# A decoder layer on one core: the samples' softmax and value products moved into the attention loop

## The chip, the cores and the metric

One core of a Trainium2 chip runs the whole kernel. The metric is the device time of one execution in microseconds (us), as the median of several; lower is better. All data are 32-bit floats. The engines are TensorE (PE), VectorE (DVE), ScalarE (ACT), GpSimd (POOL), and SyncE (SP), which only issues transfers here. Each runs its own instructions in the order written and waits on semaphores for the others.

## What is computed

One transformer layer for a prompt of 512 tokens and for 8 samples, each with one new token and a paged cache of 2048 past positions (16 pages of 128). Cut to what the change touches:

```python
proj = rmsnorm(x) @ w_in            # gates, u, v, q, k, v_c, forget
y_a = short_conv_mixer(...)         # z = c * h, three taps, gate
y_b = chunk_gmlp_mixer(...)         # layernorm(v), w_s, gate u
y_c = fox_prompt(q, k, v, logf)     # causal attention of the prompt, 8 heads, head size 64
# the samples instead attend to the cache:
s_past = einsum('nqhd,nkhd->nhqk', q, k_past) * scale + decay
s_new = einsum('nqhd,nkhd->nhqk', q, k) * scale + ...
p = softmax(concatenate([s_past, s_new]))
o = einsum(p_past, v_past) + einsum(p_new, v)
x = x + concatenate([rmsnorm(y_a), rmsnorm(y_b), rmsnorm(y_c)]) @ w_o
x = x + hier_moe(rmsnorm(x))        # 32 experts, 6 MB of weights each, top 2
x = x + (p_i @ w_ple) * sigmoid(rmsnorm(x) @ w_ple_gate)
```

## The kernel before

The program is one hand-ordered instruction list per engine. Its stages, in order:

1. **Projections and keys.** The input is normalised and transposed, and `project` (L1229, matmuls at L1237) forms half of the projections. Beside it the samples' keys are read from the cache in 32 chunks of 1 MB (128 pages, 4 key positions of 512 numbers) by indirect DMAs on GpSimd (`load_chunk`, L656, issue at L659) into a ring of six slots. Of the first `SHARED` = 24 chunks GpSimd multiplies the even ones by the query (`products`, L689) and VectorE the odd ones (`key_pair`, L1796); VectorE sums all (`reduce_keys`, L1786, instruction at L1791). Behind pairs 9 and 10 VectorE also copies the prompt's values out of PSUM (`copy_values`, L1838).
2. **Attention of the prompt.** A loop of 17 steps (`STEPS` = 16), step s working on heads 2c, 2c+1 and query block t, with c, t = s // 4, s % 4. TensorE runs `query_keys(s)` (L1318), the rest of the projections in pieces (`rest_step`, L1301, matmuls at L1313), `transpose_p(s-1)` (L1328), spreads a head's decay row over the partitions into PSUM bank 7 (`spread_ck`, L1288) or puts the values of the gating there (`spread_gv`, L1292), and at every fourth step runs `weigh_values` (L1340, matmuls at L1352) into bank 6. `CK_STEP` and `GV_STEP` say at which steps bank 7 is so used. VectorE masks and takes maxima (`negate_scores`, L1899), inverts the sums (`invert_sums`), reads bank 7 (`diagonal`, `layer_stats`, and once `layer_norms`, L1877), and sums the last eight key chunks at the steps in `REDUCE_AT`. ScalarE takes the exponentials and copies. Value chunks 0 to 3 of the cache are loaded as the four slots of the ring come free; GpSimd then builds constants and waits.
3. **Norms.** VectorE forms the convolution (`z` at L1947, taps L1954 to L1964) and the gates (L1977, L1980), TensorE the sums of squares (L1403) and the spread roots (L1413), VectorE the normalised rows (L1988). SP loads `w_o` (4 MB, L544) when the last query-key product is out and the prompt's x again (2 MB, L548) behind the last `weigh_values`.
4. **Output product, samples and routing.** `mix_out(t)` (L1450, matmuls at L1462) forms the output product of token tile t in four quarters of 4 matmuls; a matmul of 32-bit floats shows as two rows of the trace, so a quarter is 8 rows. VectorE takes the samples' softmax (L2012 to L2033) behind the norms; `values_step(i)` (L1388) forms four chunks of the samples' value product each, 8 matmuls (16 rows, L1383) into bank 7 per chunk, one accumulation over all 32 chunks. VectorE writes each chunk's probabilities, spread over the samples, into one of four buffers (`spread_p`, L2034). The load of chunk n waits for the product of chunk n - 4. `add_out` adds x, `second_norm` (L2062) takes the root on VectorE in ten instructions (`root`, L1733) and normalises, and `route(t)` (L1467) forms the routing logits. Then follow the samples' output (`oN`, L1523), the remaining tiles, the embedding product (L1567) and the lists of rows per expert.
5. **Experts.** 32 experts in a loop; SP streams each one's 6 MB into one of two buffers (L554, L555, L558). Expert 0's first 4 MB wait for the last value product, expert 1's for the last `mix_out`, the later ones for the expert before (matmuls at L1611 and L1626).
6. **Gate, last norm, stores** (matmuls at L1719).

The fills of banks 4 and 5 alternate in the order of the list `FILLS` (L86): a fill waits until the one before it in its bank is read. Bank 7 holds the decay rows in the attention and, when all are read, the sum of the value products.

## Time and profile before

| what | value |
|---|---|
| median of 3 runs | 1093.56 us (1087.73 to 1096.13) |
| profiled execution, its own time | 1092.19 us |
| its span in the trace | 1090.4 us |
| granted clock over the span | 0.896 |
| PE busy | 886.6 us (81%) |
| DVE, ACT, POOL busy | 334.0, 193.2, 264.0 us |
| HBM traffic | 297 GB/s over the span |

The span runs from the first to the last recorded instruction; 1.8 us of the execution lie around it. Times of rows count from the span's start. A PE row's clock is the share of 2.4 GHz that was granted, so 1.00 is 2.4 GHz and 0.50 is 1.2 GHz.

### The profile page before, as it was taken

The page shows a single profiled execution, that of the slowest core. Times are in us where ns is not written, and L with a number is a line of the kernel's source. Part 1 is how long each engine was busy: PE and PEld are TensorE (multiplying, and loading weights), DVE is VectorE, ACT ScalarE, POOL GpSimd, SP SyncE. Part 2 cuts the span into 40 slices and gives each one's busy share as a digit, 9 for nine tenths or more (in the row PEclk, how much of TensorE's full clock was granted, in tenths as well). Part 3 has the DMA queues.
Part 4 walks back from the last instruction along what each step waited for, and adds up shares of the span by engine and source line. Part 5 has one row for each costly group of instructions (what it writes and reads, how often), then busy time and mean ns, then how long its engine had stood idle before and what let it go on. Part 6 is the DMA issues. An engine that isn't in the chain of part 4 may idle for free.

```text
span 1090.4 us, 11578 instructions
## 1 busy us (share of the span) xinstructions
PE 886.6 (81%) x4285; PEld 465.3 (43%) x4285; DVE 334.0 (31%) x672; ACT 193.2 (18%) x391; POOL 264.0 (24%) x333
## 2 busy tenths in 40 slices
PE   5999689998697779768997787787787887885895
PEld 3888456767543335333333233333333333331342
DVE  4897456464651222460000000000000000000652
ACT  3200234544100000211101101101101101110432
POOL 6889249400012220002111111101111111001110
PEclk9999879999598898888988888988988989998898
DMA  9899526316028986705999999999999999997300
GB/s 310 320 336 372 202 95 232 119 37 243 10 83 328 399 328 238 303 5 181 404 408 415 397 402 410 409 404 413 409 412 414 405 397 413 424 404 297 150 40 38
DMA packets 53799, 316.42 MB, mean 290 GB/s; under 512 B 11214, under 2 KB 24078, under 8 KB 33016
## 3 DMA queue, kind: packets, MB, share of 16 engines
q1 hardware_dynamic: 34704, 233.28, 53.7%
q0 software_dynamic: 14480, 76.17, 18.5%
q10 hardware_dynamic: 4576, 6.46, 1.7%
q8 instruction: 24, 0.39, 0.1%
q14 instruction: 15, 0.12, 0.0%
HBM read 309.31 MB, written 14.82 MB: 297 GB/s over the span
## 4 chain that ended last, share of the span: by engine, by line
PE 48%; DMA 36%; DVE 8%; POOL 2%; issue 2%; ACT 2%; SPq 1%; POOLq 0%; DVEq 0%; ACTq 0%
DMA arena<-in_w_up 29%; PE psum L1611 14%; PE psum L1237 6%; PE psum L1719 5%; PE psum L1313 5%; PE psum L1462 5%; DMA arena<-in_cache_v,indices 4%; PE psum L1383 2%; DMA arena<-in_w_in 1%; DMA arena<-in_w_down 1%; POOL arena L692 1%; DVE arena L1791 1%; PE psum L1567 1%; PE psum L1626 1%; PE psum L1325 1%
## 5 line engine op out<-in xcount | busy, mean ns | idle before, releaser
L1611 PE MATMUL psum<-arena 128*64 128x512 f32 x1024 | 269.6, 686 | 86.4 <-DMA arena<-in_w_up 86.4
L1611 PEld LDWEIGHTS psum<-arena 128*64 128x64 f32 x1024 | 92.2, 157 | 239.7 <-issue 237.6
L2238 DVE TENSOR_TENSOR arena<-arena,psum 64x512 f32<-64x512 f32 x32 | 22.1, 692 | 385.3 <-ACT arena L1095 385.3
L1626 PE MATMUL psum<-arena 128*64 128x512 f32 x512 | 116.0, 592 | 2.1 <-DMA arena<-in_w_down 2.1
L692 POOL TENSOR_TENSOR arena<-arena 128x2048 f32<-128x2048 f32 x20 | 90.6, 4534 | 1.8 <-ACT arena L854 1.4
L1237 PE MATMUL psum<-arena 128*128 128x260 f32 x384 | 85.1, 383 | 0.2 <-DMA arena<-in_w_in 0.2
L746 POOL COPY indices<-row_list 128x1 int32 (+1 forms) x26 | 4.6, 178 | 307.0 <-ACT arena L1101 307.0
L1095 ACT ACTIVATE arena<-psum 64x512 f32<-64x512 f32 x32 | 18.8, 588 | 336.4 <-PE psum L1611 336.4
L1313 PE MATMUL psum<-arena 128*128 128x260 f32 x320 | 78.1, 398 | 0.0
L1237 PEld LDWEIGHTS psum<-arena 128*128 128x128 f32 x384 | 72.6, 190 | 12.3 <-issue 1.3
L1791 DVE TENSOR_REDUCE arena<-arena 128x32 f32<-128x2048 f32 x32 | 72.0, 2281 | 5.8 <-POOL arena L692 5.3
L1626 PEld LDWEIGHTS psum<-arena 128*64 128x64 f32 x512 | 42.0, 137 | 69.6 <-issue 68.9
L659 POOL DMA_INDIRECT arena<-in_cache_v,indices x32 | 32.2, 1006 | 158.9 <-PE psum L1383 152.3
L1313 PEld LDWEIGHTS psum<-arena 128*128 128x128 f32 x320 | 60.7, 195 | 17.4 <-issue 6.0
L1462 PE MATMUL psum<-arena 128*128 128x512 f32 x128 | 65.0, 662 | 1.8 <-DVEq L1731 1.8
L1719 PE MATMUL psum<-arena 128*128 128x512 f32 x128 | 55.7, 593 | 0.0
L747 POOL DMA_INDIRECT moe_rows<-arena,indices x32 | 32.6, 1019 | 94.8 <-ACT arena L1101 67.7
L1383 PE MATMUL psum<-arena 128*32 128x256 f32 x512 | 37.9, 441 | 18.6 <-DMA arena<-in_cache_v,indices 15.5
L659 POOL DMA_INDIRECT arena<-in_cache_k,indices x32 | 30.9, 965 | 45.5 <-DVE arena L1791 38.8
L1462 PEld LDWEIGHTS psum<-arena 128*128 128x128 f32 x128 | 26.4, 214 | 36.3 <-issue 34.2
L2242 DVE COPY arena<-psum 128x256 f32<-128x256 f32 x32 | 13.6, 425 | 86.4 <-PE psum L1619 86.4
L740 POOL DMA_INDIRECT arena<-h_rows,indices x32 | 31.2, 975 | 26.6 <-POOL indices L739 25.9
(320 smaller groups left out, 872.3 us busy)
## 6 DMA issues: line engine op xcount, KB each, us to landing
arena<-in_w_down SPq DMA_DIRECT2D x32, 2048.0 KB, 25.6
arena<-in_w_gate SPq DMA_DIRECT2D x31, 2048.0 KB, 18.3
arena<-in_w_up SPq DMA_DIRECT2D x31, 2048.0 KB, 22.8
arena<-in_w_in SPq DMA_DIRECT2D x11, 1024.0 KB, 6.9
arena<-in_x_prompt SPq DMA_DIRECT2D x8, 512.0 KB, 5.9
arena<-in_w_o SPq DMA_DIRECT2D x1, 4096.0 KB, 14.0
arena<-in_w_ple_gate SPq DMA_DIRECT2D x1, 4096.0 KB, 24.5
arena<-moe_rows SPq DMA_DIRECT2D x4, 1024.0 KB, 7.9
```

Of the source, the lines that this page charges most:

```text
L659: pool.indirect_dma_start(ring[s], None, caches[cache], bass.IndirectOffsetOnAxis(ap=chunk_ids[:, n:n + 1], axis=0)).then_inc(kv_in[s], 16)
L692: pool.tensor_tensor(r, r, q_rep, ALU.mult).then_inc(kmul, 1)
L740: pool.indirect_dma_start(h_rows[s][0:SLOTS, :], None, h2_dram, bass.IndirectOffsetOnAxis(ap=tok_ix[s][0:SLOTS, 0:1], axis=0), bounds_chec ...
L747: return pool.indirect_dma_start(moe_dram, bass.IndirectOffsetOnAxis(ap=row_ix[s][:, 0:1], axis=0), y_rows[s], None, bounds_check=2 * PAIR ...
L1237: last = mm(psum[:, 2 * q + half, 0:HALF], w_ring[s][:, k, q * P:(q + 1) * P], hT[:, k, half * HALF:(half + 1) * HALF], start=(k == 0), st ...
L1313: last = mm(bank(4 + half)[:, 0:HALF], w_ring[g % 2][:, k, q * P:(q + 1) * P], hT[:, k, half * HALF:(half + 1) * HALF], start=(k == 0), st ...
L1383: ins = mm(bank(7)[32 * g:32 * (g + 1), 0:WA], p_exp[s][:, k * HC + 4 * half:k * HC + 4 * half + 4, :], ring[s][:, k * WC + half * WA:k * ...
L1462: last = mm(bank(2 * (t % 2) + n)[0:w, :], heads, w_out[:, k, n * BANK:(n + 1) * BANK], start=(k == 0), stop=(k == DC - 1))
L1611: last = mm(bank(s)[m * SLOTS:(m + 1) * SLOTS, :], hgT[s][:, k, :], w_gu[s][m][:, k, :], start=(k == 0), stop=(k == DC - 1))
L1626: last = mm(bank(6 + s)[n * SLOTS:(n + 1) * SLOTS, :], actT[s][:, k, :], w_dn[s][:, k, n * BANK:(n + 1) * BANK], start=(k == 0), stop=(k = ...
L1719: last = mm(bank(2 * (i % 2) + n), xT[i % 2][:, k, :], w_gate_ple[:, k, n * BANK:(n + 1) * BANK], start=(k == 0), stop=(k == DC - 1))
L1791: v.tensor_reduce(scores[:, n * KEYS * HC:(n + 1) * KEYS * HC], ring[SLOT[n]].rearrange("p (a d) -> p a d", d=HD), AX.X, ALU.add).then_inc ...
```

## The change

The samples' scores are taken to their maximum at attention step 3 (VectorE), the maxima are transposed and spread at steps 5 and 6 (TensorE in bank 6, VectorE), the exponentials are at step 6 (ScalarE), the sums at step 7. The value products of chunks 0 to 19 stand in steps 10 to 15; of the 12 left, 8 stand behind the loop, 2 behind the gates and 2 ahead of the spread of the norms. The decay rows and the gating's values are through bank 7 by step 9. The probabilities of a chunk are spread over the samples in one of eight buffers, which lie where the pages' forget logs and decays were. 28 instead of 24 key chunks are summed ahead of the attention, four in it. The copies of the prompt's values stand further back on VectorE, and the new token's score (three small VectorE instructions) stands ahead of the attention. The root of the second norm moves from VectorE to GpSimd (two instructions). Cut to its core:

```diff
-SHARED = 24
-V_AFTER = {9: (0, 1), 10: (2, 3)}
-REDUCE_AT = {24: (1, 0), 25: (1, 1), 26: (2, 1), 27: (3, 0), 28: (3, 1), 29: (4, 1), 30: (5, 1), 31: (6, 0)}
+SHARED = 28
+REDUCE_AT = {28: (1, 0), 29: (1, 1), 30: (2, 1), 31: (3, 0)}
+VALUES_AT = {10: (0, 1, 2, 3), 11: (4, 5, 6, 7), 12: (8, 9, 10), 13: (11, 12, 13), 14: (14, 15, 16), 15: (17, 18, 19)}
+SPREAD_AT = {7: (0, 1, 2, 3), 10: (4, 5, 6, 7), 11: (8, 9, 10), 12: (11, 12, 13), 13: (14, 15, 16), 14: (17, 18, 19),
+             15: (20, 21, 22)}
+EXPANDED = 8
-CK_STEP = {h: 4 * (h // 2 - 1) + 1 + h % 2 for h in range(2, HC)}
-GV_STEP = {3: 0, 4: 1, 7: 2, 8: 3, 11: 4}
+CK_STEP = {2: 0, 3: 1, 4: 4, 5: 5, 6: 8, 7: 9}
+GV_STEP = {3: 0, 4: 1, 6: 2, 7: 3, 8: 4}
...
-        p_exp = [at(b_tail + 4 * SEQ + s * KEYS * HC * NB, KEYS * HC, NB) for s in range(4)]
+        p_exp = [at(pages0 + s * KEYS * HC * NB, KEYS * HC, NB) for s in range(EXPANDED)]
```

GpSimd: key chunks and first value chunks:

```diff
             for n in range(0, SHARED, 2):
                 products(n)
-                if n:
+                if 0 < n < SHARED - 4:
                     pool.wait_ge(kred, n)
                     load_chunk(0, n + 4)
                     load_chunk(0, n + 5)
             for n in range(SHARED, CHUNKS):
+                pool.wait_ge(kred, n - 3)
+                load_chunk(0, n)
+            for n in range(SHARED, CHUNKS):
                 products(n)
-                if n > SHARED:
-                    pool.wait_ge(kred, n)
-                    load_chunk((n + 3) // CHUNKS, (n + 3) % CHUNKS)
-            pool.wait_ge(kred, CHUNKS)
-            load_chunk(1, 3)
+                if n >= SHARED + 2:
+                    pool.wait_ge(kred, n - 1)
+                    load_chunk(1, n - SHARED - 2)
+            for n in (2, 3):
+                pool.wait_ge(kred, SHARED + n + 1)
+                load_chunk(1, n)
```

GpSimd, after the last value chunk's load:

```diff
+            for t in sorted(TURN, key=TURN.get):
+                w = tile_width(t)
+                r = stats[0:w, 56 + t:57 + t]
+                pool.wait_ge(x1_ms, TURN[t] + 1)
+                step(pool.tensor_scalar(r, stats[0:w, 24 + t:25 + t], 1.0 / D, EPS, ALU.mult, ALU.add))
+                pool.tensor_tensor(r, r, minus_half[0:w, :], ALU.pow).then_inc(x1_root, 1)
```

ScalarE, attention loop:

```diff
+                if s == 6:
+                    act.wait_ge(smp_exp, 1)
+                    act.activation(scores, scores, ACT.Exp).then_inc(smp_p, 1)
+                    act.wait_ge(smp_exp, 2)
+                    act.activation(pnew[0:NB, :], new_s[0:NB, :], ACT.Exp).then_inc(smp_p, 1)
```

TensorE; weigh_values(c), c > 0, also waits smp_exp 2:

```diff
+            def values(n):
+                out = bank(7)
+                if n == 0:
+                    pe.wait_ge(gv_read, TILES)
+                    pe.wait_ge(ck_diag_ready, HC)
+                    pe.wait_ge(ck_ready, HC)
+                pe.wait_ge(kv_in[SLOT[CHUNKS + n]], arrived(CHUNKS + n))
+                pe.wait_ge(px_ready, n + 1)
+                p, v = p_exp[n % EXPANDED], ring[SLOT[CHUNKS + n]]
...
+            def sample_max(rows):
+                if rows:
+                    pe.wait_ge(a_of, 1)
+                    pe.wait_ge(smp_req, 1)
+                    tr(bank(6)[0:NB, P:P + HC], new_s[0:NB, :], ident[0:NB, 0:NB])
+                    tr(bank(6)[0:HC, 0:P], max_p, ident).then_inc(smp_full, 1)
+                else:
+                    pe.wait_ge(smp_req, 2)
...
             for s in range(STEPS + 1):
...
+                if s == 5:
+                    sample_max(True)
                 if s:
                     transpose_p(s - 1)
+                for n in VALUES_AT.get(s, ()):
+                    values(n)
...
+                if s == 5:
+                    sample_max(False)
                 if s and s % QT == 0:
                     weigh_values(s // QT - 1)
...
+            values_left(len(left) - 4)
+            wait_free(pe, "sum")
+            pe.wait_ge(smp_req, 3)
+            done(mm(fill("sum")[0:NB, 0:HC], col_sel, sum_p, start=True, stop=True), "sum")
             wait_free(pe, "state")
```

After the gates:

```diff
+            values_left(2)
```

After norm_sums("normB"):

```diff
+            values_left(len(left))
             spread_norm("normC")
...
-            mix_out(0, (0, 1, 2))
-            softmax_T("maxT", 1, slice(0, HC), max_p)
-            softmax_T("maxB", 2, slice(0, P), m_exp[0:HC, :])
-            softmax_T("maxN", 2, slice(0, NB), mT[0:HC, :])
-            mix_out(0, (3,))
-            mix_out(1, (0,))
...
-            values_step(0, first=True)
-            mix_out(1, (1,))
-            values_step(1)
-            mix_out(1, (2, 3))
-            values_step(2)
+            mix_out(0)
+            mix_out(1)
             route(0)
-            for m in range(4):
-                values_step(3 + m)
-                mix_out(2, (m,))
+            mix_out(2)
             route(1)
-            values_step(7, last_one=True)
```

VectorE, ahead of the attention:

```diff
-            for n in range(5, SHARED // 2):
+            for n in range(5, SHARED // 2 - 2):
                 key_pair(n)
-                for t in V_AFTER.get(n, ()):
-                    copy_values(t)
+            multiply_keys(SHARED - 3)
+            reduce_keys(SHARED - 4)
+            copy_values(0)
+            reduce_keys(SHARED - 3)
+            copy_values(1)
+            multiply_keys(SHARED - 1)
+            copy_values(2)
+            reduce_keys(SHARED - 2)
+            copy_values(3)
+            reduce_keys(SHARED - 1)
```

VectorE, attention loop, behind negate_scores(s):

```diff
+                if s == 5:
+                    sample_max_all()
+                if s == 6:
+                    sample_subtract()
+                if s == 7:
+                    sample_sums_p()
+                for n in SPREAD_AT.get(s, ()):
+                    spread_p(n)
```

Behind invert_sums(s):

```diff
+                if s == 3:
+                    sample_max()
```

VectorE, behind the attention:

```diff
+            for n in range(max(SPREAD_AT[max(SPREAD_AT)]) + 1, CHUNKS):
+                spread_p(n)
+            wait_full(dve, "sum")
+            dve.wait_ge(smp_p, 2)
+            step(v.tensor_tensor(sum_s[0:NB, :], fill("sum")[0:NB, 0:HC], pnew[0:NB, :], ALU.add))
+            dve.nop().then_inc(free_of("sum"), 1)
+            step(v.reciprocal(sum_s[0:NB, :], sum_s[0:NB, :]))
             dve.wait_ge(half_free, rest_halves - 4)
             z = projT[:, 2:4, :]
```

VectorE, second_norm(t):

```diff
-                dve.wait_ge(x1_ms, TURN[t] + 1)
-                root(stats[0:w, 56:57], stats[0:w, 24 + t:25 + t], 1.0 / D)
+                dve.wait_ge(x1_root, TURN[t] + 1)
```

## Rows read from the trace of the kernel before

**Rows 1.** Page, part 4: the chain that ended last, by line.

```profile
DMA arena<-in_w_up 29%; PE psum L1611 14%; PE psum L1237 6%; PE psum L1719 5%; PE psum L1313 5%; PE psum L1462 5%; DMA arena<-in_cache_v,indices 4%; PE psum L1383 2%; DMA arena<-in_w_in 1%; DMA arena<-in_w_down 1%; POOL arena L692 1%; DVE arena L1791 1%; PE psum L1567 1%; PE psum L1626 1%; PE psum L1325 1%
```

**Rows 2.** Busy time by stretch: the stretches are stages 2 to 5.

```profile
core 0: us, PE busy (x) PEld busy (x) DVE busy (x) ACT busy (x) POOL busy (x), PEclk, DMA share, GB/s
143.56:264.50 120.94, 115.78 (x551) 82.99 (x550) 61.39 (x203) 59.09 (x159) 46.42 (x75) 0.96 0.37 130
264.50:297.35 32.85, 21.34 (x134) 19.62 (x132) 21.95 (x58) 5.37 (x6) 0.00 (x0) 0.62 0.24 87
297.35:411.01 113.66, 91.14 (x662) 42.16 (x663) 35.72 (x85) 6.88 (x12) 28.33 (x28) 0.87 0.71 278
495.35:998.15 502.80, 412.16 (x1905) 164.50 (x1904) 35.73 (x64) 57.72 (x96) 69.65 (x118) 0.91 0.99 399
```

**Rows 3.** Groups by line, TensorE, 297 to 411 us.

```profile
L1383 PE MATMUL psum<-arena 128*32 128x256 f32 x512 | 37.9, 441 | 18.6 <-DMA arena<-in_cache_v,indices 15.5 <-DVE arena L2038 3.1
```

**Rows 4.** Timeline, TensorE: start, duration, line, shape, count, [idle before and releaser].

```profile
297.35 13.31 PE L1462 MATMUL psum<-arena 128*128 128x512 f32 x24 [1.78 <-DVEq L1731]
...
322.73 3.70 PE L1462 MATMUL psum<-arena 128*128 128x512 f32 x8
326.42 1.07 PE L1383 MATMUL psum<-arena 128*32 128x256 f32 x16
...
333.83 1.93 PE L1383 MATMUL psum<-arena 128*32 128x256 f32 x16 [2.63 <-DMA arena<-in_cache_v,indices]
...
403.13 1.95 PE L1482 MATMUL psum<-arena 128*128 128x36 f32 x16 [0.90 <-ACTq L1036]
```

**Rows 5.** Timeline, VectorE, ahead of the attention.

```profile
98.57 4.48 DVE L1791 TENSOR_REDUCE arena<-arena 128x32 f32<-128x2048 f32 x2
121.57 0.69 DVE L1840 COPY arena<-psum 128x512 f32<-128x512 f32 x1 [18.52 <-PE psum L1245]
...
124.01 2.29 DVE L1800 TENSOR_TENSOR arena<-arena,psum 128x2048 f32<-128x2048 f32 x1 [0.24 <-DVE arena L1840]
...
140.76 0.69 DVE L1894 SCALAR_TENSOR_TENSOR arena<-psum,arena 128x512 f32<-128x512 f32 x1
```

**Rows 6.** Timeline, TensorE, attention step 4.

```profile
179.41 3.98 PE L1352 MATMUL psum<-arena 128*64 128x512 f32 x16 [1.92 <-ACT arena L952]
```

**Rows 7.** Busy time by stretch: attention steps 10 and 16.

```profile
217.47:223.50 6.03, 6.03 (x27) 4.05 (x26) 2.52 (x11) 3.52 (x11) 0.00 (x0) 1.00 0.55 172
256.91:264.50 7.59, 6.85 (x42) 4.86 (x40) 0.00 (x0) 3.44 (x7) 0.00 (x0) 1.00 1.02 414
```

**Rows 8.** Timeline, SyncE's transfers: issue time, time in issue, line.

```profile
252.78 0.37 SPq L544 DMA_DIRECT2D arena<-in_w_o  x1
```

**Rows 9.** Timeline, VectorE, the norms.

```profile
255.54 1.22 DVE L1947 TENSOR_TENSOR arena<-arena 128x1040 f32<-128x1040 f32 x1
264.95 0.49 DVE L1956 TENSOR_SCALAR arena<-arena 128x520 f32<-128x520 f32 x1 [8.19 <-PE psum L1419]
...
275.71 0.69 DVE L1977 TENSOR_TENSOR arena<-psum,arena 128x512 f32<-128x512 f32 x1 [3.08 <-PE psum L1440]
...
278.95 0.68 DVE L1992 TENSOR_TENSOR arena<-arena 8x512 f32<-8x512 f32 x1
```

**Rows 10.** Timeline, TensorE, the norms.

```profile
267.21 5.60 PE L1403 MATMUL psum<-arena 128*128 128x1 f32 x32 [2.17 <-ACT arena L983]
...
280.01 3.57 PE L1403 MATMUL psum<-arena 128*128 128x1 f32 x16 [1.02 <-ACT arena L1001]
...
283.80 3.78 PE L1413 MATMUL psum<-arena 128*128 128x128 f32 x16
```

**Rows 11.** Timeline, VectorE, root and second norm of the samples' tile.

```profile
443.74 0.14 DVE L1738 TENSOR_SCALAR arena<-arena 8x1 f32<-8x1 f32 x1 [1.21 <-ACT arena L1019]
...
445.88 1.27 DVE L2068 SCALAR_TENSOR_TENSOR arena<-arena 8x1024 f32<-8x1024 f32 x1
```

**Rows 12.** One line's instructions: GpSimd's power at L641, min/median/max ns.

```profile
L641 POOL TENSOR_TENSOR arena<-arena x5: 553/556/857, 7.1 to 15.4; 128x1 f32<-128x1 f32 x4, 8x1 f32<-8x1 f32 x1
```

More of the change, by code:

```diff
@@ L88 @@
          + ["suffix"]
-         + ["state", "vnT", "z", "gate0", "gate1"]
-         + ["newT", "normC", "normA", "normB", "maxT", "maxB", "maxN"]
-         + ["sum"] + [f"h{t}{s}" for t in (0, 1) for s in "abr"] + ["oN", "oT"] + [f"h2{s}" for s in "abr"] + ["normS"]
+         + ["sum", "state", "vnT", "z", "gate0", "gate1", "normC", "normA", "normB"]
+         + [f"h{t}{s}" for t in (0, 1) for s in "abr"] + ["oN", "oT"] + [f"h2{s}" for s in "abr"] + ["normS"]
          + ["p01", "p23", "p4"] + [f"h{t}{s}" for t in (4, 3) for s in "abr"]
@@ L232, in build @@
         params_nat = small(P)
+        pages0 = small_top[0]
         logf_pages = small(PAGE, HC)
@@ L1354, in weigh_values @@
                 last.then_inc(a_o, 1)
+            def values(n):
[7 more added lines that the diff above has]
+                p, v = p_exp[n % EXPANDED], ring[SLOT[CHUNKS + n]]
+                for k in range(KEYS):
+                    for half in range(2):
+                        g = 2 * (k % 2) + half
+                        ins = mm(out[32 * g:32 * (g + 1), 0:WA], p[:, k * HC + 4 * half:k * HC + 4 * half + 4, :],
+                                 v[:, k * WC + half * WA:k * WC + (half + 1) * WA],
+                                 start=(n == 0 and k < 2), stop=(n == CHUNKS - 1 and k >= 2), skip_group_check=True)
+                ins.then_inc(pv_done, 1)
+            def sample_max(rows):
[6 more added lines that the diff above has]
+                    pe.wait_ge(smp_req, 2)
+                    tr(bank(6)[:, 0:HC], m_exp[0:HC, :], ident[0:HC, 0:HC])
+                    tr(bank(6)[0:NB, P:P + HC], mT[0:HC, :], ident[0:HC, 0:HC]).then_inc(smp_full, 1)
             spread_ck(0)
@@ L1371, in _ @@
                     spread_gv(GV_STEP[s])
+                if s == 5:
+                    sample_max(False)
                 if s and s % QT == 0:
                     weigh_values(s // QT - 1)
-            def values(s, loaded, spread, first=False, last_one=False):
-                pe.wait_ge(kv_in[s], loaded)
-                pe.wait_ge(px_ready, spread)
-                for k in range(KEYS):
-                    for half in range(2):
-                        g = 2 * (k % 2) + half
-                        ins = mm(bank(7)[32 * g:32 * (g + 1), 0:WA], p_exp[s][:, k * HC + 4 * half:k * HC + 4 * half + 4, :],
-                                 ring[s][:, k * WC + half * WA:k * WC + (half + 1) * WA],
-                                 start=(first and k < 2), stop=(last_one and k >= 2), skip_group_check=True)
-                ins.then_inc(pv_done, 1)
-            def values_step(i, **flags):
-                for s in range(4):
-                    values(s, arrived(CHUNKS + 4 * i + s), 4 * i + s + 1, flags.get("first", False) and s == 0,
-                           flags.get("last_one", False) and s == 3)
             pe.wait_ge(a_pt, 2 * STEPS)
@@ L1415, in spread_norm, with values_left @@
                 done(last, name)
+            left = list(range(max(VALUES_AT[max(VALUES_AT)]) + 1, CHUNKS))
+            def values_left(n):
+                for _ in range(n):
+                    values(left.pop(0))
+            values_left(len(left) - 4)
+            wait_free(pe, "sum")
+            pe.wait_ge(smp_req, 3)
+            done(mm(fill("sum")[0:NB, 0:HC], col_sel, sum_p, start=True, stop=True), "sum")
             wait_free(pe, "state")
@@ L1442, in _ @@
                 done(last, name)
-            def softmax_T(name, need, dst, src):
-                wait_free(pe, name)
-                pe.wait_ge(smp_req, need)
-                n = src.shape[0]
-                done(tr(fill(name)[dst, 0:n], src, ident[0:n, 0:n]), name)
+            values_left(2)
             def mix_out(t, quarters=(0, 1, 2, 3)):
@@ L1860, in _ @@
             dve.nop().then_inc(free_of("suffix"), 1)
+            for name in ("ks", "vs"):
+                dve.wait_ge(free_of(name), AT[name][1] + 1)
+            step(v.tensor_tensor(prod_s[0:NB, :], q_s[0:NB, :], k_s[0:NB, :], ALU.mult))
+            step(v.tensor_reduce(new_s[0:NB, :], prod_s[0:NB, :].rearrange("p (h d) -> p h d", h=HC), AX.X, ALU.add))
+            step(v.tensor_tensor(new_s[0:NB, :], new_s[0:NB, :], f_nat[0:NB, QT, :], ALU.subtract))
             step(v.memset(mv, 1.0))
```

116 lines of the change are left out of this document (43 added, 73 removed).

## The prediction

> **What bounds the kernel now.** I read the page's chain first. Its largest item is the transfer of the experts' weights, with the experts' matmuls behind it [rows 1]. The table of stretches says the same: over 502.8 us the DMA engines are busy 0.99 of the time at 399 GB/s, so the expert stage is a stream of 201 MB that nothing in this change touches [rows 2]. It starts when the routing lists are there, so a gain ahead of it moves the whole rest forward by its own size, and nothing else counts. Ahead of it the same table shows three stages of different kinds. In the attention TensorE is busy 115.8 of 120.9 us and DMA only 0.37. In the norms neither is full: 21.3 of 32.9 us and a granted clock of 0.62. In the output product, up to the samples' output, TensorE has 91.1 of 113.7 us at a DMA share of 0.71 [rows 2]. The groups by line say why: TensorE waited 15.5 us directly for value chunks and 3.1 us for VectorE ahead of the value products, and the chain gives these transfers 4% of the span, some 43 us [rows 1, 3]. So 32 chunks of 1 MB are loaded and used in a stage where they are the bound, while the DMA engines idle in the two stages before. The change moves them there. The question is how much TensorE and the transfers lose on the way.
>
> All sums are in the coordinates of the profiled execution (1092.19 us), which is 1.4 us under the median shown; I take the forecast made against it as the forecast of the median.
>
> **1. Ahead of the attention: -5.4 us.** VectorE ends key pair 9 at 103.05 us and then waits 18.5 us for the prompt's first transposed values; the first decay row is read at 140.76 [rows 5]. After the change two pairs' work stands in that gap. A pair is one product of 2.29 and a double sum of 4.48, 6.77 us [rows 5]. Pairs 10 and 11 end at 116.6, one product and one sum (2.24) at 121.1, just when the values come (121.57). Behind them come four copies of 0.69, three sums of 2.24 and one product, 11.8 us, to 133.4; page_suf 0.2; the new token's score, three instructions that took from 278.95 to 280.5 us, 1.55 [rows 9]; the memset 0.1. The decay row is read at 135.3 instead of 140.8. GpSimd's products are paced by the same pairs as now and hold nothing up; ScalarE's stores need the fourth copy, at 131 us, and are done by then.
>
> **2. Attention up to step 9: -1.5 us.** TensorE waits 1.92 us at step 4, behind VectorE, which waits for GpSimd's late key chunks [rows 6]. With four chunks left instead of eight, and GpSimd free of loads between their products, I let this and a smaller wait beside it go, -2.5. Four small transposes of the samples' maxima cost +1. The softmax adds to VectorE at step 3 about 4.5 us, at steps 5 to 7 some 5 us, and 32 spreads of 0.42 us; it loses four sums of 2.28. VectorE is busy 61.4 of 120.9 us [rows 2] and TensorE asks for each step's result a step later, so I take nothing; its other end is one late step, +3. The exponential on ScalarE (1 us, half idle there) is hidden too. GpSimd's building of constants stood in its long wait and moves ahead with the value loads, still ahead of step 10.
>
> **3. Steps 10 to 15: +21.4 us.** A chunk's product takes 1.07 us at the full clock [rows 4]; 20 of them are 21.4 us on an engine without gaps (step 10: 6.03 of 6.03 us, [rows 7]). Do the chunks arrive? Four lie ready. The DMA queue gave 414 GB/s when full [rows 7], so a chunk takes 2.53 us. Step 11 wants four chunks in some 11 us and the others three in 8 to 11 us, 7.6 us of transfer: they do. The ends are 0 and +6, a wait of 1 to 2 us in some steps for the first chunk of a refill. I take 0. So the last weigh_values ends at 264.6 - 5.4 - 1.5 + 21.4 = 279, I say 280.
>
> **4. The eight chunks behind the loop: done at 298.** This is where I expect the transfers to become late. w_o now goes out at 252.8 [rows 8], then at 252.8 - 6.9 + 17 x 1.07 = 264. The load of chunk n waits for product n - 4, so chunks 21 to 23 go out from 270 on. From 270 to the landing of chunk 27 the queue has to move the rest of w_o (4.2 MB less 5.5 us x 0.414 = 1.9 MB), chunks 21 to 27 (7.3 MB) and x (2.1 MB, out at 280): 11.3 MB, 27.4 us at 414 GB/s, so 297.4. TensorE alone would be through at 280 + 8 x 1.07 = 288.6. These are the ends if the value chunks went ahead of the others or came last. The profile shows the value loads only without such company. I take the late end, 298. The Trainium skill, "DMA: Bandwidth & Descriptors" (Queues, rings and completion order), says that each DMA engine serves its queues in turn, packet by packet; by that x and w_o land within the same stretch and the late end holds. The same page (Where 436 GB/s comes from) puts the HBM side at about 358 GB/s per core; the row with 414 disagrees, and by the page the time here would be 31.6 us, 4 us more.
>
> **5. From there to the output product: +38 us.** VectorE now gets to z only behind the sum of the exponentials, which TensorE forms behind chunk 27. So z, ready at 256.8 and hidden, moves onto the path: about 0.3 + 0.5 + 1.22 = 2 us [rows 9]. From the first tap (264.95) to mix_out (297.35) it is 32.4 us now [rows 4, 9]. Off go the new token's score, 1.55, and most of the 3.08 us that the gates waited for TensorE [rows 9], since its 5.60 us of sums [rows 10] now start before the taps. On come four chunks between the gates and the spread norms, on a TensorE that takes its sums of squares, 3.57 us, and the spread in turn [rows 10]: 4.3 us at the full clock, 7.7 at the half one, as the 1.93 us of a chunk behind a wait show [rows 4]; the stage runs at 0.62 [rows 2]. 2 + 32.4 - 1.5 - 2.9 + 4.3 = 34.3, or with the half clock for chunks and sums about 41; I take 38. The output product starts at 336 instead of 297.35: +38.7.
>
> **6. The output product: -57.2 us.** It is 113.66 us now [rows 2]. What stays: the first three quarters 13.31, nine quarters at 3.65 (a row shows 3.70) = 32.9, two routes of 4.0 (transposes 1.0, wait 0.90, product 1.95, [rows 4]). New is a wait ahead of the samples' output: VectorE reads bank 7 only behind add_out(2), the logits and the second norm, which the last four chunks covered; 1.28 + 0.42 and the hops, 2.3 us. Sum 56.5.
>
> **7. The root on GpSimd: -1.3 us.** The samples' tile waits on it ahead of its routing: VectorE takes 445.88 - 443.74 = 2.14 us [rows 11], GpSimd a power of 0.56 and a smaller instruction of 0.2 [rows 12]. The next tile's root lies behind the same path and gains no more. GpSimd waits for nothing else there.
>
> **The sum:** +38.7 - 57.2 - 1.3 = -19.8 us (points 1 to 4 are in the 336), 1092.2 - 19.8 = 1072.4. **1072 us**, its own range 1066 to 1080.
>
> **The rivals.** *The transfers are not late* (20%): chunks 21 to 27 get through ahead of w_o and x, TensorE ends chunk 27 at 289 and the norms take 34 to 36. 1072 less 9 to 13: 1061. For it: at step 10 DMA is at 0.55 [rows 7], over the whole attention at 0.37 [rows 2]. Against it: w_o and x must move in the same 30 us.
>
> *The value loads cost the attention too* (20%): four slots with a round trip through TensorE, GpSimd and the queue leave 1 to 2 us at each of steps 11 to 15, +6, and the norm stage runs at the half clock, +3, with 2 to 3 us of VectorE's softmax on the path. 1084. For it: chunk products waited 2.63 and more behind a refill in the old order [rows 4], on a full queue. A change that fails to do what it says would look so as well: products placed early that stand waiting.
>
> *Slower* (5%): the waits in steps 10 to 16 take TensorE to its half clock, and the projections and transposes there pay double. That stretch is 47 us with 44 of TensorE work, so at the half clock +44 us; the gain of 20 is gone when the clock is down in more than 45% of it, and for all of it the time is 1116. For it: the stages in which TensorE waits for others run at 0.62 and 0.87, the attention at 0.96 [rows 2]. Against it: the projections keep TensorE busy 4 us and more per step whatever the chunks do. The Trainium skill, "TensorE: Matmul & The Clock Gate" (What's actually happening), says that the throttled clock is the default and activity releases it; the norm stage's 0.62 agrees.
>
> The forecast has the remaining 55%. A measurement of this kernel tells about 1%, 11 us, from no change. Faster by over 1% (under 1081): the forecast nearly whole, the first rival, a little of the second, 0.77. Within 1%: most of the second, 0.18. Slower 0.05. The range reaches from the first rival to the second: 1059 to 1086.
>
> **What would show it.** Right: in the attention no wait of TensorE ahead of a value product over 2 us, the last weigh_values ending near 280; waits of TensorE for in_cache_v of 5 to 12 us in total, nearly all behind the loop; chunk 27 near 298; mix_out near 336 and then some 57 us to the samples' output with no value product in it; the expert stage again 503 us at 399 GB/s. Wrong: chunk 27 before 291 (point 4), a norm stage under 34 or over 42 (point 5), a wait of more than 4 us ahead of the samples' output (point 6), or a clock under 0.9 in steps 10 to 15 (the slower rival).

## The result and the profile after

The changed kernel takes 1099.54 us (median of 13 runs, 1095.66 to 1103.11) against 1093.56 us for the kernel before (now also 13 runs, 1087.73 to 1099.41): a ratio of 1.0052, 95% interval 1.0032 to 1.0072. So it is about 6 us slower, a change of half a per cent, where 1072 was forecast with a range of 1059 to 1086. The profiled execution took 1103.11 us with a span of 1101.3, at the top of its own runs; the stretches below are compared with the 1090.4 us span of before.

The same kind of table as [rows 2], for the kernel after: start to attention, attention, value chunks behind it, norms, output product up to the samples' part, routing, the bulk of the experts, the end.

```profile
core 0: us, PE busy (x) PEld busy (x) DVE busy (x) ACT busy (x) POOL busy (x), PEclk, DMA share, GB/s
0.00:152.80 152.80, 117.51 (x571) 92.81 (x571) 128.53 (x93) 23.88 (x43) 120.20 (x84) 0.91 0.86 312
152.80:303.20 150.40, 138.42 (x879) 93.80 (x882) 68.48 (x237) 60.58 (x161) 40.19 (x86) 0.94 0.52 194
303.20:330.30 27.10, 13.43 (x131) 4.72 (x131) 1.70 (x4) 2.51 (x2) 6.77 (x7) 0.59 1.02 421
330.30:367.76 37.46, 28.02 (x200) 22.66 (x194) 21.86 (x57) 2.86 (x4) 0.94 (x1) 0.59 0.49 198
367.76:421.24 53.48, 49.77 (x144) 24.56 (x145) 8.28 (x11) 5.62 (x10) 2.25 (x6) 0.95 0.08 30
421.24:504.10 82.86, 64.15 (x272) 34.60 (x274) 34.82 (x107) 14.28 (x26) 6.74 (x14) 0.81 0.34 132
504.10:1008.00 503.90, 415.06 (x1904) 162.85 (x1904) 35.72 (x64) 57.76 (x96) 69.81 (x118) 0.90 0.99 398
```

The output product is done in 53.48 us where it took 113.66 [rows 2], as meant. But the product now starts at 367.76 instead of 297.35. Four things stand ahead of it: the attention starts at 152.8 where it started at 143.56 and was to start at 138; it takes 150.4 us; 27.1 us of value chunks follow, at a DMA share of 1.02; and the norms take 37.5 us where they took 32.9. The expert stage is the same stream as before, 503.9 us at 398 GB/s.

**Where the start went.** VectorE, from the last key reduction to the first decay row that it reads (timeline: start, duration, engine, line):

```profile
132.84 2.29 DVE L1804 TENSOR_REDUCE arena<-arena 128x32 f32<-128x2048 f32 x1 [0.24 <-DVE arena L1856]
135.05 0.16 DVE L1883 TENSOR_TENSOR arena<-psum,arena 128x8 f32<-128x8 f32 x1
135.43 0.69 DVE L1888 TENSOR_TENSOR arena<-arena 8x512 f32<-8x512 f32 x1 [0.22 <-DVEq L1884]
136.15 0.67 DVE L1889 TENSOR_REDUCE arena<-arena 8x8 f32<-8x512 f32 x1
136.86 12.92 DVE L1890 TENSOR_TENSOR arena<-arena 8x8 f32<-8x8 f32 x1
...
149.95 0.69 DVE L1924 SCALAR_TENSOR_TENSOR arena<-psum,arena 128x512 f32<-128x512 f32 x1
```

Down to L1889 the order and the durations are those forecast, some 2 us late in all. Then a subtraction of 8x8 numbers, the last of the new token's score, takes 12.92 us. It shows as busy, not as idle before: no semaphore was awaited. GpSimd in the same stretch:

```profile
135.40 0.94 POOL L661 DMA_INDIRECT arena<-in_cache_k,indices  x1 [2.19 <-DVE arena L1804]
136.35 13.41 POOL L694 TENSOR_TENSOR arena<-arena 128x2048 f32<-128x2048 f32 x3
```

It computes three key products from 136.35 to 149.76, and the subtraction ends at 149.78. The two score instructions that began ahead of 136.35 took 0.69 and 0.67. The Trainium skill, "SBUF — State Buffer" (SBUF: two separate sides), says that GpSimd and VectorE share one pair of SBUF ports as an exclusive lock, which whichever starts first holds for its whole instruction, and that a VectorE operation with two inputs in SBUF is blocked so by a GpSimd operation that reads SBUF. The trace agrees that the subtraction, begun 0.5 us behind the first product, stood. But by one whole instruction it would have been free after some 4.5 us (13.41 / 3), and it stood through all three products.

**What stayed late.** TensorE behind the last attention step (in brackets the idle time before and its releaser):

```profile
300.81 2.37 PE L1362 MATMUL psum<-arena 128*64 128x512 f32 x16 [0.74 <-ACT arena L961]
303.12 1.93 PE L1379 MATMUL psum<-arena 128*32 128x256 f32 x32
308.26 1.93 PE L1379 MATMUL psum<-arena 128*32 128x256 f32 x16 [3.21 <-DMA arena<-in_cache_v,indices]
313.40 1.93 PE L1379 MATMUL psum<-arena 128*32 128x256 f32 x16 [3.21 <-DMA arena<-in_cache_v,indices]
317.30 1.94 PE L1379 MATMUL psum<-arena 128*32 128x256 f32 x16 [1.97 <-DMA arena<-in_cache_v,indices]
320.98 1.94 PE L1379 MATMUL psum<-arena 128*32 128x256 f32 x16 [1.75 <-DMA arena<-in_cache_v,indices]
324.69 1.93 PE L1379 MATMUL psum<-arena 128*32 128x256 f32 x16 [1.77 <-DMA arena<-in_cache_v,indices]
328.39 1.94 PE L1379 MATMUL psum<-arena 128*32 128x256 f32 x16 [1.77 <-DMA arena<-in_cache_v,indices]
```

Chunks 20 and 21 go through at once, then each of the six chunks up to 27 waits for its rows, 13.7 us in all. The page's group for all 32 chunks, beside the 18.6 us of [rows 3]:

```profile
L1379 PE MATMUL psum<-arena 128*32 128x256 f32 x512 | 39.1, 455 | 14.8 <-DMA arena<-in_cache_v,indices 14.8
```

So the waiting for value rows is nearly what it was, 14.8 against 15.5 us; the change moved it from the output product to the end of the loop. What shares the DMA engines there is in SyncE's issues (a3 tries whether it is the reason):

```profile
288.48 0.37 SPq L546 DMA_DIRECT2D arena<-in_w_o  x1
303.23 1.76 SPq L550 DMA_DIRECT2D arena<-in_x_prompt  x4
```

The output weights were 32.3 us on the way (the page's list of issues), beside the value rows and x.

**The attention.** Three waits of TensorE that were not there before or were shorter:

```profile
190.28 0.69 PE L1307 MATMUL psum<-arena 128*128 128x128 f32 x2 [2.98 <-DVEq L1744]
224.01 0.38 PE L1307 MATMUL psum<-arena 128*8 128x128 f32 x2 [1.64 <-DVEq L1744]
245.60 2.08 PE L1334 MATMUL psum<-arena 64*128 64x512 f32 x4 [4.72 <-DVE arena L1943]
```

In front of the last one VectorE does all tiles' layer norms in one block and only then step 10's negated maxima (L1941, L1943), for which step 11's query-key product (L1334) waits. After the wait this product takes 2.08 us where a full clock gives 1.13.

The other two stand ahead of `spread_gv` (L1307), which puts the gating's values into bank 7, at steps 4 and 8. With the new `CK_STEP` and `GV_STEP` a decay row goes into the same bank earlier in these two steps; in the kernel before no step had both. So the row must first be copied by ScalarE and then be read by VectorE. At step 8:

```profile
219.30 1.12 PE L1299 MATMUL psum<-arena 8*128 8x512 f32 x2
222.69 0.48 ACT L926 ACTIVATE arena<-psum 128x384 f32<-128x384 f32 x1
223.21 0.69 DVE L1924 SCALAR_TENSOR_TENSOR arena<-psum,arena 128x512 f32<-128x512 f32 x1 [5.59 <-ACT arena L926]
```

VectorE stood idle for 5.59 us before it read the row, so the samples' softmax has no part in this wait. At step 4 it has one: VectorE's block for the samples' maxima (179.97 to 184.48) makes that step's own maxima late, ScalarE's exponentials (186.37) follow them, and its copy of the row (188.96) follows those. The `weigh_values` behind that wait took 4.54 us, those of steps 8 and 12 took 2.37.

### The profile page after: what moved, and what is told of

Its sections match the earlier page's. It is cut to its first block, busy times and chain, and to the rows that moved or that the text cites. A ratio compares the mean times of both kernels' runs of the same rounds, so it can differ in the third digit from the quotient of the medians.

```text
span 1101.3 us, 11534 instructions
## 1 busy us (share of the span) xinstructions
PE 892.3 (81%) x4285; PEld 465.9 (42%) x4285; DVE 339.3 (31%) x624; ACT 193.5 (18%) x391; POOL 258.6 (23%) x341
## 4 chain that ended last, share of the span: by engine, by line
PE 49%; DMA 35%; DVE 9%; issue 3%; ACT 2%; SPq 1%; POOL 0%; POOLq 0%; DVEq 0%; ACTq 0%
DMA arena<-in_w_up 28%; PE psum L1624 13%; PE psum L1246 8%; PE psum L1732 5%; PE psum L1322 5%; PE psum L1494 5%; DMA arena<-in_cache_v,indices 4%; DMA arena<-in_w_down 2%; PE psum L1379 2%; PE psum L1639 1%; DVE arena L1890 1%; PE psum L1580 1%; PE psum L1334 1%; PE psum L1514 1%; PE psum L1362 1%
## 5 line engine op out<-in xcount | busy, mean ns | idle before, releaser
L1246 PE MATMUL psum<-arena 128*128 128x260 f32 x384 | 86.5, 388 | 0.0
L694 POOL TENSOR_TENSOR arena<-arena 128x2048 f32<-128x2048 f32 x18 | 81.5, 4537 | 2.3 <-ACT arena L867 1.1
L1322 PE MATMUL psum<-arena 128*128 128x260 f32 x320 | 79.6, 402 | 0.0
L1104 ACT ACTIVATE arena<-psum 64x512 f32<-64x512 f32 x32 | 18.9, 589 | 337.3 <-PE psum L1624 337.3
L1494 PE MATMUL psum<-arena 128*128 128x512 f32 x128 | 60.7, 634 | 1.8 <-DVEq L1744 1.8
L1732 PE MATMUL psum<-arena 128*128 128x512 f32 x128 | 55.7, 593 | 0.0
L1379 PE MATMUL psum<-arena 128*32 128x256 f32 x512 | 39.1, 455 | 14.8 <-DMA arena<-in_cache_v,indices 14.8
L1615 PE MATMUL psum<-arena 64*128 64x64 f32 x256 | 35.0, 278 | 1.9 <-ACT arena L1082 1.1
## 6 DMA issues: line engine op xcount, KB each, us to landing
arena<-in_w_o SPq DMA_DIRECT2D x1, 4096.0 KB, 32.3
```

Of the source, the lines that this page charges most:

```text
L694: pool.tensor_tensor(r, r, q_rep, ALU.mult).then_inc(kmul, 1)
L1246: last = mm(psum[:, 2 * q + half, 0:HALF], w_ring[s][:, k, q * P:(q + 1) * P], hT[:, k, half * HALF:(half + 1) * HALF], start=(k == 0), st ...
L1322: last = mm(bank(4 + half)[:, 0:HALF], w_ring[g % 2][:, k, q * P:(q + 1) * P], hT[:, k, half * HALF:(half + 1) * HALF], start=(k == 0), st ...
L1379: ins = mm(out[32 * g:32 * (g + 1), 0:WA], p[:, k * HC + 4 * half:k * HC + 4 * half + 4, :], v[:, k * WC + half * WA:k * WC + (half + 1) * ...
L1494: last = mm(bank(2 * (t % 2) + n)[0:w, :], heads, w_out[:, k, n * BANK:(n + 1) * BANK], start=(k == 0), stop=(k == DC - 1))
L1615: last = tr(bank(4)[:, k * SLOTS:(k + 1) * SLOTS], hv[0:SLOTS, k, :], ident[0:SLOTS, 0:SLOTS])
```

## The experiments

Four theories, one for each loss: (a) the 8x8 subtraction is held by GpSimd; (b) value rows and output weights share one bandwidth behind the loop; (c) the remaining value chunks and the norms stand one behind the other although they don't depend on each other; (d) the block of layer norms makes step 10 late. The first four kernels ran together on one chip (before: 1095.43 us, 23 runs), the last four on another (before: 1093.24 us, 13 runs). Gains over the change are differences of ratios to before, times 1093.6 us. With the intervals of both ratios each gain is known to some 3 to 5 us.

| kernel | ratio to before, 95% | less than after | start of attention | its length | loop end to output product |
|---|---|---|---|---|---|
| after | 1.0052 (1.0032 to 1.0072) | | 152.8 | 150.4 | 64.6 |
| a1, score early | 0.9925 (0.9902 to 0.9948) | 13.9 us | 137.4 | 149.7 | 64.2 |
| a2, operand in PSUM | 0.9937 (0.9911 to 0.9962) | 12.6 us | 139.6 | 149.9 | 63.7 |
| a3, output weights late | 0.9964 (0.9943 to 0.9984) | 9.6 us | 150.0 | 150.3 | 53.9 |
| a4, chunks between norms | 0.9834 (0.9794 to 0.9874) | 23.8 us | 152.3 | 150.1 | 40.4 |
| b4, layer norms split | 1.0033 (1.0010 to 1.0056) | 2.1 us | 151.6 | 146.8 | 64.4 |
| b1, a1 and a3 | 0.9862 (0.9827 to 0.9897) | 20.8 us | 139.8 | 149.9 | 51.8 |
| b2, a1 and a4 | 0.9736 (0.9701 to 0.9771) | 34.6 us | 138.0 | 150.7 | 38.2 |
| b3, a1, a4 and b4 | 0.9712 (0.9676 to 0.9748) | 37.2 us | 139.8 | 147.9 | 38.8 |

The last three columns are us from each kernel's trace: the first product of step 0, the end of the last weigh_values less that, and from there to the first product with the output weights. The first column of them varies by up to 3 us between executions with nothing changed ahead of it.

**a1: the score ahead of the last key reduction.**

```diff
+            for name in ("ks", "vs"):
+                dve.wait_ge(free_of(name), AT[name][1] + 1)
+            step(v.tensor_tensor(prod_s[0:NB, :], q_s[0:NB, :], k_s[0:NB, :], ALU.mult))
+            step(v.tensor_reduce(new_s[0:NB, :], prod_s[0:NB, :].rearrange("p (h d) -> p h d", h=HC), AX.X, ALU.add))
+            step(v.tensor_tensor(new_s[0:NB, :], new_s[0:NB, :], f_nat[0:NB, QT, :], ALU.subtract))
             reduce_keys(SHARED - 1)
             wait_full(dve, "suffix")
             step(v.tensor_tensor(page_suf, fill("suffix")[:, 0:HC], decay[:, PAGE - 1, :], ALU.add))
             dve.nop().then_inc(free_of("suffix"), 1)
-            for name in ("ks", "vs"):
...
```

> The three VectorE instructions of the new token's score (product, reduction, 8x8 subtraction) stand ahead of the last key reduction instead of behind the suffix addition, as they did before the change: at that point GpSimd computes nothing. Theory 'GpSimd and VectorE exclude each other': the 8x8 subtraction took 12.92 us because GpSimd ran its three key products at the same time; moved, it takes 0.15 to 0.7 us, the first decay row is read near 137 us instead of 149.95, the attention loop starts about 12.5 us earlier, and the whole is 10 to 13 us shorter than after the change (about 1087). Rival 'the instruction waited for its own data (the decay column or the request's values)': it then stands as long in the new place, only earlier in the row, and blocks the last key reduction; no gain. Rival 'the gain is eaten behind the loop', because the value loads, not the attention, set when the first value product can run: the loop ends 12 us earlier and the last value chunk less than 5 us earlier.

VectorE's timeline:

```profile
130.35 0.68 DVE L1883 TENSOR_TENSOR arena<-arena 8x512 f32<-8x512 f32 x1 [0.32 <-DVEq L1857]
131.06 0.67 DVE L1884 TENSOR_REDUCE arena<-arena 8x8 f32<-8x512 f32 x1
131.77 0.15 DVE L1885 TENSOR_TENSOR arena<-arena 8x8 f32<-8x8 f32 x1
131.96 2.29 DVE L1804 TENSOR_REDUCE arena<-arena 128x32 f32<-128x2048 f32 x1
...
134.60 0.69 DVE L1923 SCALAR_TENSOR_TENSOR arena<-psum,arena 128x512 f32<-128x512 f32 x1
```

The subtraction takes 0.15 us, the decay row is read at 134.6 (forecast: 135.3), and the whole gains 13.9 us (10 to 13 expected). It did not wait for its data, and the gain is not eaten behind the loop: loop end to output product is 64.2 us as before it.

**a2: the same place, one operand in PSUM.**

```diff
+            raw = bank(3)[0:NB, 0:HC]
-            step(v.tensor_reduce(new_s[0:NB, :], prod_s[0:NB, :].rearrange("p (h d) -> p h d", h=HC), AX.X, ALU.add))
-            step(v.tensor_tensor(new_s[0:NB, :], new_s[0:NB, :], f_nat[0:NB, QT, :], ALU.subtract))
+            step(v.tensor_reduce(raw, prod_s[0:NB, :].rearrange("p (h d) -> p h d", h=HC), AX.X, ALU.add))
+            step(v.tensor_tensor(new_s[0:NB, :], raw, f_nat[0:NB, QT, :], ALU.subtract))
```

> Same place as after the change, under the same three GpSimd key products, but the reduction writes its 8x8 result to PSUM and the subtraction reads that operand from PSUM, the other from SBUF. Theory 'a VectorE instruction with both inputs in SBUF is held while a GpSimd product runs, one with an input in PSUM is not': the subtraction takes under 1 us, the first decay row is read near 138 us, and the whole is as long as with the three instructions moved (10 to 13 us below after the change). Rival 'the place is what costs' (a wait for data, or VectorE held by any GpSimd product whatever its operands): the subtraction still takes about 13 us and the time is that of after.

VectorE's timeline:

```profile
134.99 0.69 DVE L1888 TENSOR_TENSOR arena<-arena 8x512 f32<-8x512 f32 x1 [0.22 <-DVEq L1884]
135.71 0.68 DVE L1890 TENSOR_REDUCE psum<-arena 8x8 f32<-8x512 f32 x1
136.43 0.15 DVE L1891 TENSOR_TENSOR arena<-psum,arena 8x8 f32<-8x8 f32 x1
```

In its old place, with one operand in PSUM, the subtraction takes 0.15 us, while GpSimd's three products run from 135.92 to 149.36. Together with a1 this settles theory (a): neither place nor data but the pair of SBUF inputs beside GpSimd's products.

**a3: output weights issued when 28 chunks are multiplied.**

```diff
             sp.wait_ge(gv_full, TILES)
+            sp.wait_ge(pv_done, CHUNKS - 4)
             sp.dma_start(w_out, a["w_o"][0].rearrange("(k p) n -> p k n", p=P)).then_inc(w_o_in, 16)
```

> SyncE issues the load of the output weights (and what stands behind it in its queue) only when 28 of the 32 value chunks have been multiplied. After the change it was issued at 288.5 us and took 32.3 us to land, and the value rows came at half the pace beside it (PE waited 1.8 to 3.2 us ahead of each chunk, chunk 27 was done 27.1 us behind the loop, at 420 GB/s in all). Theory 'the two transfers share one bandwidth': chunk 27 is done 7 to 11 us earlier, the weights land late but still ahead of the mix that needs them (37 us of norms lie between), and the whole is 6 to 10 us shorter. Rival 'half clock and products, not the transfers, set the pace': the chunks stay near 1.9 us each and the gain is under 3 us. Rival 'the weights become what is late': PE waits for them ahead of the mix, and the gain of the chunks is lost.

TensorE behind the loop:

```profile
300.31 3.72 PE L1380 MATMUL psum<-arena 128*32 128x256 f32 x64
307.97 1.79 PE L1380 MATMUL psum<-arena 128*32 128x256 f32 x16 [3.95 <-DMA arena<-in_cache_v,indices]
310.94 1.94 PE L1380 MATMUL psum<-arena 128*32 128x256 f32 x16 [1.18 <-DMA arena<-in_cache_v,indices]
313.41 1.83 PE L1380 MATMUL psum<-arena 128*32 128x256 f32 x16 [0.54 <-DMA arena<-in_cache_v,indices]
315.90 1.07 PE L1380 MATMUL psum<-arena 128*32 128x256 f32 x16 [0.66 <-DMA arena<-in_cache_v,indices]
```

Four chunks go through at once, four wait 6.3 us in all; chunk 27 is done 16.6 us behind the loop instead of 27.1. The weights land 19.8 us after their issue, in the norms. Theory (b) holds, with one limit: SyncE issues in order, so the prompt's x went out behind the weights, at 317.5 instead of 303.2 us. The edit took both loads, 6.3 MB, from beside the value rows, and no run parts them.

**a4: chunks between the norms.** The order of TensorE behind the loop, in short:

```diff
-            values_left(len(left) - 4)
+            values_left(2)
...
             done(last, "vnT")
+            values_left(1)
             norm_sums("normC")
+            values_left(1)
...
             norm_sums("normA")
+            values_left(1)
             norm_sums("normB")
-            values_left(len(left))
             spread_norm("normC")
+            values_left(1)
             spread_norm("normA")
+            values_left(1)
             spread_norm("normB")
+            values_left(1)
...
-            mix_out(0)
+            mix_out(0, (0, 1))
+            values_left(1)
+            mix_out(0, (2, 3))
+            values_left(1)
             mix_out(1)
```

Two more stand behind z and the gates, and the samples' sum follows the last spread. VectorE's last spreads of the probabilities move along, one or two at a place.

> Nothing of the norms of the gated output depends on the samples' values, apart from the last scaling. The value chunks that are left behind the loop stand in this kernel between the parts of the norm stage and between the output products of the first half, two or fewer at each place, and the sum of the samples' weights is taken behind them. Theory 'after the change the values and the norm stage stand one behind the other (27.1 + 37.5 us from the end of the loop to the mix), and the norm stage is a chain between engines in which PE waits': interleaved, the mix starts 15 to 25 us earlier (near 345 us instead of 367.8), less what the value chunks add to it, and the whole is 12 to 22 us shorter. Rival 'the transfers hold it': the value rows arrive no earlier, PE waits for them at the new places with the norms behind it, and the gain is under 6 us.

```profile
316.77 1.93 PE L1379 MATMUL psum<-arena 128*32 128x256 f32 x16
...
319.58 1.47 PE L1379 MATMUL psum<-arena 128*32 128x256 f32 x16
320.98 1.97 PE L1477 MATMUL psum<-arena 128*64 128x128 f32 x32
322.87 1.07 PE L1379 MATMUL psum<-arena 128*32 128x256 f32 x16
...
339.76 1.16 PE L1440 MATMUL psum<-arena 128*128 128x128 f32 x8 [3.78 <-DVEq L1753]
340.85 1.92 PE L1379 MATMUL psum<-arena 128*32 128x256 f32 x16
...
342.70 7.93 PE L1494 MATMUL psum<-arena 128*128 128x512 f32 x16
```

Of the six waits for value rows behind the loop one is left (3.31 us), and five of the ten chunks placed singly take 1.07 us, the full clock. From loop end to output product it is 40.4 us instead of 64.6. At 23.8 us this is the largest loss, a little above the 12 to 22 expected, and the product starts at 342.7 (near 345 expected). The output weights still go out at 287.6 and take 33 us: with the chunks spread over the norms they cost no more than that one wait. The edit does several things at once (the chunks between the norms, two of them inside the output product, the samples' sum off the path to z), and no run parts these.

**b4: layer norms one tile per step.**

```diff
-                if s == max(GV_STEP) + 1:
-                    layer_norms()
+                if 0 < s - max(GV_STEP) <= TILES:
+                    layer_norms((s - max(GV_STEP) - 1,))
```

> The layer norms of the four tiles of the prompt's values, which stand as one VectorE block (233.8 to 243.7 us after the change) ahead of the negated maxima of attention step 10, are taken one tile per step in steps 9 to 12 instead. After the change PE waited 4.72 us there and worked at half clock behind it (a 2.08 us product where 1.13 us is usual). Theory 'the block is what makes step 10 late': the 4.72 us wait goes or falls under 1.5 us, the products behind it stay at full clock, and the whole is 4 to 7 us shorter than after the change. Rival 'only moved': later steps wait in its place, since the softmax rows of VectorE stay the tighter chain there, and the gain is under 2 us. Rival 'the value loads set the end of the value products anyway': the loop ends earlier, but chunk 27 does not.

```profile
239.43 1.13 PE L1334 MATMUL psum<-arena 64*128 64x512 f32 x4
...
246.50 1.07 PE L1379 MATMUL psum<-arena 128*32 128x256 f32 x16 [0.58 <-DMA arena<-in_cache_v,indices]
248.93 1.07 PE L1379 MATMUL psum<-arena 128*32 128x256 f32 x16 [1.36 <-DMA arena<-in_cache_v,indices]
251.42 1.07 PE L1379 MATMUL psum<-arena 128*32 128x256 f32 x16 [1.41 <-DMA arena<-in_cache_v,indices]
```

The wait of 4.72 us is gone and step 11's query-key product is back at 1.13 us, but the value chunks of that step, now earlier, wait 3.35 us for their rows. The attention is 3.6 us shorter. The ratio is 2.1 us below that of after, with intervals that overlap, so the timing alone does not show a gain; the attention's length does, and b3 repeats it (147.9 against b2's 150.7; in time 2.6 us, again with intervals that overlap). The 4 to 7 us expected were missed: the result lies next to the rival "only moved". Theory (d) holds for the wait; but of its cost, 4.72 us of waiting and 2.2 us of half clock (2.08 and 5.00 us where b4 has 1.13 and 3.77), only 3.6 us is gained; the rest came back as waits for value rows.

**b1, b2 and b3: together.** Each consists of the edits above.

> Score early and output weights late together. Each alone took 12.95 and 8.85 us off the change's time. Theory 'two independent causes': the gains add to about 22 us (1078), with chunk 27 done 13 us behind the loop (it was 27 us with the weights early, in both kernels). Rival 'both gain from the same wait for value rows': the loop ends earlier, the value rows do not come earlier, and chunk 27 is done more than 20 us behind the loop; the sum is then under 15 us.

> Score early and the value chunks between the norms. Alone they took 12.95 and 22.97 us off the change's time. Theory 'independent': about 36 us together, 1064. Rival 'the value rows come no earlier': the chunks at the first places between the norms wait for their rows by as much as the loop ends earlier, and the sum is 23 to 28 us (1072 to 1076).

> Score early, value chunks between the norms, and the layer norms one tile per attention step. If the three are independent, 36 us and another 4 to 6 us off the change's time: 1058 to 1060, some 3 per cent below the kernel before the change. If the transfers are what is left, no more than with two of them (1064).

b1 gains 20.8 us where the two alone give 23.5, and chunk 27 is done 18.6 us behind the loop. The "13 us" of the expectation was counted from the fourth chunk; counted from the end of weigh_values a3 has 16.6, so b1 stands 2 us above independence and 1.4 us short of the rival's 20; its gain is far from the rival's 15. b2 gains 34.6 where the sum is 37.7. Both shortfalls, 2.7 and 3.1 us, are within what the gains are known to. b3 is the fastest kernel here, 1060.26 us, 2.9% below the kernel before (0.9676 to 0.9748). Its stretch from the end of the loop to the output product:

```profile
core 0: us, PE busy (x) PEld busy (x) DVE busy (x) ACT busy (x) POOL busy (x), PEclk, DMA share, GB/s
287.70:326.47 38.77, 32.37 (x292) 23.18 (x293) 21.80 (x58) 5.38 (x6) 7.58 (x8) 0.75 0.93 380
```

TensorE has work in 32.4 of 38.8 us behind the loop and the DMA engines in 0.93 of it: in the change TensorE had work in 13.4 of the 27.1 us of the chunks, and the DMA engines in 0.49 of the norms.

## Why the prediction was wrong, step by step

Forecast and profiled execution differ by 1103.1 - 1072.4 = 30.7 us. Its steps account for it.

- **Point 1 failed: +14.6 us.** I had priced the score's three instructions at 1.55 us from their old place behind the attention [rows 9], where GpSimd does nothing (its busy time in the norm stage is 0.00, [rows 2]). I had moved them, in my sum, to a stretch in which GpSimd multiplies keys, had asked only what VectorE's queue does, and had written of GpSimd's products that they "hold nothing up". They held one of the three for 12.92 us. The duration of a row holds for the neighbours it was taken beside. a1 and a2 give 13.9 and 12.6 us back.
- **Points 2 and 3 were low: +8.6 us** (280 - 138.2 = 141.8 forecast, 150.4 measured). The claim about the chunks was right: the waits for rows inside the loop sum to 1.2 us. Their products even took 18.9 us where I had 21.4, since four in a row take 3.66. So the other terms missed by some 11 us. The bound that I had named and taken as nothing, "one late step, +3", came three times, 2.98, 1.64 and 4.72 us. The last is VectorE's block of layer norms ahead of step 10's maxima, with products at half clock behind it (b4). The first two come where a decay row and the gating's values now share bank 7 in one step. I had priced the new steps of the decay rows at nothing, without a reason; the samples' softmax has a part in the wait of step 4 only. I also expected the wait of step 4 [rows 6] to go, where 2.98 and 0.74 took its place. This reading of steps 4 and 8 is from the timeline and was not tried.
- **Point 4 failed in size: +9.1 us.** The mechanism was right: the transfers become late, all of them in one queueing stretch at 421 GB/s. But I had let the weights move 2.3 MB alone first and then counted seven chunks (21 to 27) beside them and x, 11.3 MB. From the weights' issue to the landing of chunk 27, 288.5 to 328.4, the DMA engines moved 14.7 us x 0.402 + 25.2 us x 0.421 = 16.5 MB (402 GB/s is what the table of stretches gives for 288.48 to 303.20); without the weights and x, 6.3 MB, that is nearly ten chunks, 18 to 27. Nothing moved alone. It took 27.1 us behind the loop, not 18, and TensorE's waits for value rows were 14.8 us, not 5 to 12. a3 shows the part of the weights and x, 10.5 us of it.
- **Point 5 was right:** 37.46 us against 38, and the four chunks in it took 6.7 us, between the 4.3 and 7.7 that I had. But it was right about a thing that I had accepted as given. The eight chunks behind the loop and the norms don't depend on one another, and I added them as 18 + 38. a4 shows that adding them up, not a term, was what cost most: 24 us.
- **Point 6 was right:** 53.48 against 56.5; the wait ahead of the samples' output is 1.92 us (2.3 forecast).
- **Point 7 was right:** from there to the experts 82.86 us, before 84.34 (495.35 - 411.01), -1.5.
- The experts and the end are 2.1 us longer, within what executions differ by.

Together 14.6 + 8.6 + 9.1 - 0.5 - 3.0 - 0.2 + 2.1 = 30.7 us.

Of the rivals the second, "the value loads cost the attention too", comes nearest once the lock is taken out: a1's ratio gives 1085 us, the rival 1084. That its price fits is luck, its cause was mostly not there: the attention lost its time to waits for VectorE and bank 7, not to loads. The rival that ends slower named the clock in steps 10 to 16. There the granted clock was 0.95 (232.23 to 303.18 us), over the 0.9 set as the sign, so that isn't what happened; half the clock cost about 2.2 us behind the wait ahead of step 11. None of the rivals had one instruction held by another engine.

## What to carry to other kernels

When a small VectorE instruction is moved, look at what GpSimd does at the new place: with both inputs in SBUF it may stand as long as GpSimd's queue of products is, and it shows as a long busy time of a tiny tile, not as a wait. Writing one operand to PSUM, or moving the score ahead of the last key reduction, cost nothing here and gave 13 us. When a buffer's uses are moved between steps, look for steps that now use it twice: each such step waits for the engines that must read it in between (2.98 and 1.64 us here). When a stage bound by transfers is moved next to one bound by a chain between engines, interleave the two in the instruction order; put one behind the other and each leaves the other's resource idle (24 us here). And ask of each bulk load what it shares the DMA engines with at its new issue time.

## What the runs showed of the hardware

- An 8x8 VectorE subtraction with both inputs in SBUF was held for 12.92 us (12.92 in a3 and a4, 12.93 in b4) across three GpSimd instructions, not one: it did not get in between them. With one operand in PSUM it took 0.15 us under the same products. So did other operations beside them: the decay rows' scalar_tensor_tensor with one input in PSUM (0.69 us at 138.03 in a1), and reciprocals of one SBUF input (0.16 us at 139.84).
- The DMA engines moved 421 GB/s over 27.1 us from GpSimd's and SyncE's queues together, and served them side by side: a 4 MB load took 32.3 us when issued beside the value rows, 19.8 and 18.4 us when issued behind all but the last four chunks (a3, b1).
- In the changed kernel a product of one value chunk took 1.07 us in the attention, where the granted clock was 0.94, and 1.93 us behind the loop, where TensorE waited 1.75 to 3.21 us ahead of each and the clock was 0.59.
